# A weight ring of sixteen 1 MB units in place of eight units of 2 MB

## The reference

```
p = h @ w_in                                   # 1024 x 2560
mix = concat(attention(q, k, v), gated spatial mix, causal conv(31) + LN + silu) @ w_out   # 1024 x 1024
h = LayerNorm(alpha * h + mix)
for e in range(16):                            # top-1 group of experts, then top-2 experts of it
    out += gates[:, e:e+1] * ((silu(h @ w_gate[e]) * (h @ w_up[e])) @ w_down[e])
h = LayerNorm(alpha * h + out)
```

## Time and profile before

| | us |
|---|---|
| median of 3 runs (lowest, highest) | 730.11 (729.67, 730.49) |
| the profiled execution | 730.29 |
| its span, first to last instruction | 728.4 |
| TensorE matmul busy | 668.5 |
| VectorE busy | 281.4 |
| ScalarE busy | 141.3 |

### The profile page before, as it was taken

One profiled execution on the slowest core, in us unless ns is written; L12 is line 12 of the kernel. 1 busy time (PEld: TensorE's weight loads), 2 busy tenths in 40 slices (PEclk: granted clock), 3 DMA queues, 4 the chain that ended last, 5 costly groups with the idle time before them and its releaser, 6 DMA issues.

```text
span 728.4 us, 7319 instructions
## 1 busy us (share of the span) xinstructions
PE 668.5 (92%) x3007; PEld 327.9 (45%) x3007; DVE 281.4 (39%) x585; ACT 141.3 (19%) x280; POOL 67.9 (9%) x65
## 2 busy tenths in 40 slices
PE   7999998799999999887689999979999999997882
PEld 5644586443333543232375447846333345332331
DVE  4496668310323022130627937770120330320226
ACT  2102463131110220010121026522201122110100
POOL 1603000510000000000050310006000000000000
PEclk9999999899999999999979999998999999999997
DMA  8999535089999999999999532333999999999981
GB/s 283 345 388 416 243 119 229 1 354 409 423 422 421 421 422 420 423 420 422 393 386 405 232 142 96 136 117 142 379 421 422 421 422 422 420 422 422 421 360 60
DMA packets 48572, 240.72 MB, mean 330 GB/s; under 512 B 4428, under 2 KB 8852, under 8 KB 23956
## 3 DMA queue, kind: packets, MB, share of 16 engines
q1 hardware_dynamic: 47380, 235.97, 80.5%
q10 hardware_dynamic: 1152, 4.19, 1.5%
HBM read 239.10 MB, written 1.05 MB: 330 GB/s over the span
## 4 chain that ended last, share of the span: by engine, by line
PE 66%; DMA 18%; DVE 10%; issue 3%; POOL 2%; ACT 1%; DVEq 0%; POOLq 0%
PE bank L534 22%; PE bank L553 12%; PE bank L455 11%; DMA ring<-in_w_up 9%; DMA ring<-in_w_gate 8%; PE bank L512 5%; PE bank L469 5%; DVE mix L1278 3%; PE bank L573 3%; PE bank L610 2%; PE bank L542 1%; PE bank L682 1%; PE bank L433 1%; DVE stats L1204 1%; DVE h L1197 1%
## 5 line engine op out<-in xcount | busy, mean ns | idle before, releaser
L534 PE MATMUL bank<-ring,xe 128*64 128x512 f32 x1024 | 226.4, 594 | 18.3 <-DMA ring<-in_w_up 10.5
L534 PEld LDWEIGHTS bank<-ring,xe 128*64 128x64 f32 x1024 | 71.4, 137 | 166.6 <-issue 134.5
L553 PE MATMUL bank<-ring,area_b 128*64 128x512 f32 x512 | 113.4, 595 | 1.6 <-DVE area_b L1217 1.6
L1211 DVE TENSOR_TENSOR area_b<-area_b,bank 128x512 f32<-128x512 f32 x16 | 11.0, 688 | 261.1 <-PE bank L534 261.1
L455 PE MATMUL bank<-ring,xT_area 128*128 128x512 f32 x256 | 111.3, 593 | 0.0
L455 PEld LDWEIGHTS bank<-ring,xT_area 128*128 128x128 f32 x256 | 48.1, 190 | 57.4 <-issue 57.4
L553 PEld LDWEIGHTS bank<-ring,area_b 128*64 128x64 f32 x512 | 35.3, 137 | 68.3 <-issue 64.0
L937 POOL TENSOR_TENSOR rstd<-var_eps,half_neg 128x1 f32<-128x1 f32 x18 | 11.7, 658 | 551.9 <-DVE var_eps L1024 551.9
L1231 DVE SCALAR_TENSOR_TENSOR y_lo<-bank,slot_gate,y_hi 128x512 fp32r<-128x512 f32 x32 | 24.0, 751 | 89.1 <-ACT y_hi L858 89.1
L1278 DVE SCALAR_TENSOR_TENSOR mix<-glu,tapsT,mix 128x256 f32<-128x256 f32 x120 | 47.7, 475 | 0.0
L858 ACT ACTIVATE y_hi<-bank,slot_gate 128x512 fp32r<-128x512 f32 x32 | 22.0, 687 | 98.1 <-PE bank L553 98.1
(11 more groups left out here) (159 smaller groups left out, 568.4 us busy)
## 6 DMA issues: line engine op xcount, KB each, us to landing
ring<-in_w_gate SPq DMA_DIRECT2D x32, 2048.0 KB, 23.6
ring<-in_w_up SPq DMA_DIRECT2D x32, 2048.0 KB, 25.2
ring<-in_w_down SPq DMA_DIRECT2D x32, 2048.0 KB, 26.4
ring<-in_w_in SPq DMA_DIRECT2D x9, 2048.0 KB, 21.1
ring<-in_w_out SPq DMA_DIRECT2D x4, 2048.0 KB, 22.0
ring<-in_w_in SPq DMA_DIRECT2D x2, 1024.0 KB, 7.1
h<-in_x SPq DMA_DIRECT2D x2, 512.0 KB, 3.7
ln_par<-in_ln_mix_g ACTq DMA_DIRECT2D x2, 512.0 KB, 8.1
```

The costliest lines, as they stand in the source:

```text
L534: mm = pe.matmul(bank[2 + u % 2][e * SLOTS:(e + 1) * SLOTS, :], xe[:, k, at + e * SLOTS:at + (e + 1) * SLOTS], w[:, e, c, :], start=k == 0 ...
L553: mm = pe.matmul(bank[5 + n][e * SLOTS:(e + 1) * SLOTS, :], hidT[:, k, e * SLOTS:(e + 1) * SLOTS], w[:, e, c, n * BANK:(n + 1) * BANK], st ...
```

## The change

The unit becomes 1 MB (`UNIT = 2048`) and the ring sixteen of them; the ring's bytes stay. Each slab is two units (chunks 0 to 3 and chunks 4 to 7), each expert unit of before two units of 1024 adjacent floats for each expert and partition: 256 runs of 4 KB in each. All transfers, waits and releases are by these units, in the same order of bytes but for the second half of a slab of `w_out`, which is loaded first, as it is used first. The first slab comes in four transfers in place of two. Within `down`, units of two chunks are in use side by side, and each is released after its last product.

```diff
-UNIT = 4096
-RING = 8
-SLABS = 5 + 2
-PAIR_UNITS = 6
+UNIT = 2048
+RING = 16
+SLABS = 2 * (5 + 2)
+PAIR_UNITS = 12
...
+                to = [unit_at(n + k).rearrange("p (c n) -> p c n", c=KC // 2) for k in range(2)]
+                of = [src[:, KC // 2 * k:KC // 2 * (k + 1), :] for k in range(2)]
                 if n == 0:
-                    sp.dma_start(dst[:, :, CV:], src[:, :, CV:]).then_inc(first_half_in, 16)
-                    sp.dma_start(dst[:, :, 0:CV], src[:, :, 0:CV]).then_inc(landed[0], 16)
-                else:
-                    sp.dma_start(dst, src).then_inc(landed[n % RING], 16)
+                    for k in range(2):
+                        sp.dma_start(to[k][:, :, CV:], of[k][:, :, CV:]).then_inc(first_half_in, 16)
+                    for k in range(2):
+                        sp.dma_start(to[k][:, :, 0:CV], of[k][:, :, 0:CV]).then_inc(landed[k], 16)
+                    return
+                for k in (0, 1) if i < 5 else (1, 0):
+                    if n >= RING:
+                        sp.wait_ge(used, n - RING + (1 if i < 5 and k == 0 else 2))
+                    sp.dma_start(to[k], of[k]).then_inc(landed[(n + k) % RING], 16)
...
-                        half = u // 2 if u < 4 else u - 4
-                        if u < 4:
-                            w = (w_gate, w_up)[u % 2][l].rearrange("e (p c) n -> p e (c n)", c=KC)
+                        part = 2 * (u // 4) + u % 2 if u < 8 else u - 8
+                        if u < 8:
+                            w = (w_gate, w_up)[u // 2 % 2][l].rearrange("e (p c) n -> p e (c n)", c=KC)
                         else:
                             w = w_down[l].rearrange("e (p c) n -> p e (c n)", c=FC)
-                        src = w[:, bass.ds(first, 2), half * 2048:(half + 1) * 2048]
+                        src = w[:, bass.ds(first, 2), part * 1024:(part + 1) * 1024]
...
-                wait_unit(pe, n)
-                w = unit_at(n).rearrange("p (c n) -> p c n", c=KC)
                 for c in range(KC):
-                    mm = pe.matmul(dst[:, :], xT[:, c, b * P:(b + 1) * P], w[:, c, :],
+                    u = n + c // 4
+                    if c % 4 == 0:
+                        wait_unit(pe, u)
+                    mm = pe.matmul(dst[:, :], xT[:, c, b * P:(b + 1) * P], unit_at(u)[:, c % 4 * BANK:(c % 4 + 1) * BANK],
                                    start=c == 0, stop=c == KC - 1)
+                    if b == TB - 1 and c == 3:
+                        mm.then_inc(used, 1)
...
-                    for u in range(4):
-                        if j % GROUP == 0 and u == 2:
+                    for u in range(8):
+                        if j % GROUP == 0 and u == 4:
                             gather(g, range(4, KC))
-                        w = landed_unit(PAIR_UNITS * j + u).rearrange("p (e c n) -> p e c n", e=2, c=4)
-                        for c in range(4):
+                        w = landed_unit(PAIR_UNITS * j + u).rearrange("p (e c n) -> p e c n", e=2, c=2)
+                        for c in range(2):
...
-                    for u in range(2):
-                        w = landed_unit(PAIR_UNITS * j + 4 + u).rearrange("p (e c n) -> p e c n", e=2, c=2)
+                    for u in range(0, FC, 2):
+                        w = [landed_unit(PAIR_UNITS * j + 8 + u).rearrange("p (e n) -> p e n", e=2), None]
                         for n in range(2):
                             for c in range(2):
+                                k = u + c
+                                if n == 0 and c == 1:
+                                    w[1] = landed_unit(PAIR_UNITS * j + 8 + k).rearrange("p (e n) -> p e n", e=2)
                                 for e in range(2):
...
+                                if n == 1:
+                                    mm.then_inc(ps.used, 1)
...
-                        mm.then_inc(ps.used, 1)
```

More of the change, by code:

```diff
@@ L282, in __init__ @@
                 self.main = name == "main"
+                self.landing = 16 if self.main else 32
                 self.rounds = rounds
@@ L297, in trunk @@
             more_used = sem(f"more{l}_used")
-            more_landed = [sem(f"more{l}_landed{i}") for i in range(RING)]
+            more_both = [sem(f"more{l}_landed{i}") for i in range(RING // 2)]
+            more_landed = [more_both[i // 2] for i in range(RING)]
             o = Pass("more", more_used, more_landed, l * LAYER_UNITS + SLABS, RING, 0, ROUNDS - 1)
@@ L382, in _ @@
                 main, more = passes[l]
-                for i in range(SLABS):
-                    load_slab(l, i, l * LAYER_UNITS + i)
+                for i in range(SLABS // 2):
+                    load_slab(l, i, l * LAYER_UNITS + 2 * i)
                     if l == 0 and i == 0:
@@ L470, in product @@
                                    start=k0 == 0 and k == 0, stop=k0 == KC - 1 and k == 2)
-                    if k0 == KC - 1 and b == 0 and k == 0:
+                    if k0 == KC - 1 and b == 0 and k < 2:
                         mm.then_inc(used, 1)
@@ L495, in landed_unit @@
                     at = (ps.unit0 + k) % RING
-                    turns = rnd * (ITERS * TURNS * 16) + it * (TURNS * 16)
-                    pe.wait_ge(ps.landed[at], turns + 16 * ((ps.load0 + k) // RING + 1))
+                    turns = rnd * (ITERS * TURNS * ps.landing) + it * (TURNS * ps.landing)
+                    pe.wait_ge(ps.landed[at], turns + ps.landing * ((ps.load0 + k) // RING + 1))
                     return ring[:, at, :]
@@ L524, in gate_up @@
                     g, at = j // GROUP, (j % GROUP) * P
-                    for u in range(4):
-                        if j % GROUP == 0 and u == 2:
+                    for u in range(8):
+                        if j % GROUP == 0 and u == 4:
                             gather(g, range(4, KC))
-                        w = landed_unit(PAIR_UNITS * j + u).rearrange("p (e c n) -> p e c n", e=2, c=4)
-                        for c in range(4):
-                            k = 4 * (u // 2) + c
-                            if j % GROUP == 0 and u % 2 == 0:
+                        w = landed_unit(PAIR_UNITS * j + u).rearrange("p (e c n) -> p e c n", e=2, c=2)
+                        for c in range(2):
+                            k = 4 * (u // 4) + 2 * (u % 2) + c
+                            if j % GROUP == 0 and u // 2 % 2 == 0:
                                 nth_group("xe", g, k + 1, KC)
                             for e in range(2):
-                                mm = pe.matmul(bank[2 + u % 2][e * SLOTS:(e + 1) * SLOTS, :],
+                                mm = pe.matmul(bank[2 + u // 2 % 2][e * SLOTS:(e + 1) * SLOTS, :],
                                                xe[:, k, at + e * SLOTS:at + (e + 1) * SLOTS], w[:, e, c, :],
@@ L601, in _ @@
                 wait_xT(l, 0, TB - 1)
-                w = unit_at(u0).rearrange("p (c n) -> p c n", c=KC)
                 for k in (2, 3, 0, 1):
                     if l == 0 and k == 2:
-                        pe.wait_ge(first_half_in, 16)
-                    elif k == (2, 0)[l == 0]:
-                        wait_unit(pe, u0)
+                        pe.wait_ge(first_half_in, 32)
                     for c in range(KC):
+                        if k == (2, 0)[l == 0] and c % 4 == 0:
+                            wait_unit(pe, u0 + c // 4)
                         mm = pe.matmul(bank[4 + k // 2][:, (k % 2) * SEQ:(k % 2 + 1) * SEQ],
-                                       w[:, c, k * P:(k + 1) * P], xT[:, c, :], start=c == 0, stop=c == KC - 1)
+                                       unit_at(u0 + c // 4)[:, c % 4 * BANK + k * P:c % 4 * BANK + (k + 1) * P], xT[:, c, :],
+                                       start=c == 0, stop=c == KC - 1)
+                        if k == 1 and c == 3:
+                            mm.then_inc(used, 1)
                 mm.then_inc(used, 1)
@@ L614, in _ @@
                     setup()
-                rows_slab(u0 + 1, (0, 1))
+                rows_slab(u0 + 2, (0, 1))
                 if l == 0:
                     pe.wait_ge(setup_copied, 1)
-                rows_slab(u0 + 2, (2, 3))
+                rows_slab(u0 + 4, (2, 3))
                 pe.wait_ge(conv_step, CB * TAPS * (l + 1))
@@ L625, in _ @@
                 mm.then_inc(convT_pe, 1)
-                rows_slab(u0 + 3, (6, 7))
+                rows_slab(u0 + 6, (6, 7))
                 pe.wait_ge(rot_done, 2 * TB * (l + 1))
@@ L675, in _ @@
                 mm.then_inc(spatial_pe, 1)
-                block_slab(u0 + 4, 1, bank[5])
+                block_slab(u0 + 8, 1, bank[5])
                 for g in range(6):
@@ L786, in w_high @@
             def w_high(l, i):
-                n = l * LAYER_UNITS + 5 + i // KC
-                if i % KC == 0:
+                c = OUT_CHUNKS[i % KC]
+                n = l * LAYER_UNITS + 10 + 2 * (i // KC) + c // 4
+                if i % 4 == 0:
                     act.wait_ge(landed[n % RING], 16 * (n // RING + 1))
```

(8 more changed lines are left out.)

26 lines of the change are left out of this document (11 added, 15 removed).

## The result

The changed kernel takes 737.70 us (median of 5 runs, 737.15 to 738.20) against 730.34 for the kernel before: ratio 1.0107, 95% interval 1.0093 to 1.0121. The forecast was 736.5, and slower. The profiled execution took 737.6 with a span of 735.7 us; before it was 730.29 and 728.4.

A forecast was written before the change was run, and what follows sets the result against it. TensorE paces the mixer and first five expert pairs, the weight stream each layer's last two. Rate +5.8 and start -1.75 move the last landing +4.0; down ends +3.1, twice +6.2: 730.29 to 736.5 us, range 731.0 to 741.5.

The forecast's parts named there:

- The stream without a pause: Each layer's expert weights from unit 10 on: 38 units back to back, whose start and rate fix the layer's end.
- the term counted twice: Down's end in each layer moves from 356.28 to 359.4, +3.1 us, once per layer: +6.2.
- The rate: Expert weight stream with 4 KB runs: 2 MB take 5.13 us in place of 4.98, +5.8 us a layer.
- The line through two saturated neighbours: Per-packet plus per-byte cost, from 8 KB at 421 and 2 KB at 386 GB/s: 4 KB at 408.6 GB/s.
- The start of the stream: Early in each layer's experts, smaller units are released sooner, so the unpaused stream begins 1.75 us earlier.
- The tail: Last down: last MB lands at 356.6, three of four quarters remain, 2.65 plus 0.2 us; down ends at 359.4.
- SyncE's issues: Twice as many, 0.37 us each, hidden while the queue is filled: nothing; uncovered, 0.37 at a start, twice.
- the first slab: Program start: two more issues of 0.65 us ahead of the sg_w load cost nothing, 1.3 us if wrong.
- TensorE's added waits: At unit boundaries in the experts: more waits cost nothing where the data is there.
- near five transfers: SyncE's queue depth: about 23.6 / 4.98 transfers held, the same number of packets after the change.
- a sign against it: Everything up to layer 0's experts stays unmoved; a first 135 us that moved would prove the forecast wrong.
- The sum: Whole kernel: profiled 730.29 + 6.2 = 736.5 us, range 731.0 to 741.5; this case's chance 0.80.

The follow-up runs named there:

- the second time: The changed kernel run and profiled once more with no edit: 737.40 us, ratio 1.0110 to the kernel before.
- runs_8k: Changed kernel's 1 MB units, but one expert each in 8 KB runs, waited for and released two together: 729.87 us, ratio 1.0001 to the kernel before.
- runs_4k: 1 MB units of one expert, waits and releases two together, against the same with 8 KB runs: runs cut to 4 KB; 746.21 us.
- runs_2k: 1 MB units of one expert, waits and releases two together: gate and up in 2 KB runs, down in 4 KB; 756.46 us.
- runs_16k: Kernel before, 2 MB units, but 28 of each layer's 38 stream units hold one expert's whole matrix in 16 KB runs: 727.05 us, ratio 0.9965.
- coarse_waits: Changed kernel's transfers, but TensorE waits for and releases the experts' units two at a time: 741.55 us, ratio 1.0157 to the kernel before.
- halves: Kernel before, but four units per layer (one early, last three) come in two 1 MB transfers of 4 KB runs: 729.44 us, ratio 0.9991.

## Why the prediction was right

*What bounds it, and the unit of account.* Right. The stream without a pause and its rate set both layers' ends; the term counted twice (+3.7 and +3.2 of expert time, and +4.0 and +3.6 the second time, for +3.1 each).

*The rate.* The line through two saturated neighbours gave 408.6 GB/s and 2.566 us for 1 MB; the windows show 409 and the landings 2.56. runs_8k shows that the number of transfers has no part in it, runs_4k and runs_2k that the run's length alone does it, the 426 of runs_16k that the line goes on. By coarse_waits the term is +5.1 to +5.3 a layer for the 5.5 to 5.8 of units 10 to 45 or 47.

*The start of the stream.* This is the term that was mis-sized. The releases moved by 1.7 us as reckoned, but not the stream's end. In coarse_waits the last MB of up weights lands 205.9 us after the first gate_up (348.06 - 142.13), in the changed kernel 205.2 (348.76 - 143.57); both profiles of the changed kernel have 205.2 and 205.5 in layer 0 and 204.7 and 205.2 in layer 1, coarse_waits 205.9 and 205.8, so 0.4 to 1.1 us reach the end of the stream, 0.7 in the mean, not 1.75. In halves 1.7 at the request left 0.1 at the landing. The sum had the stream at full rate from its first packet; in the windows the units that are asked for one at a time, as they are released, move more slowly (354 GB/s in halves against 404). How much of the changed kernel's missing 1 us this makes is not shown.

*The tail.* The landing to wait for was the predicted one, with 12 of 32 instructions left, and the last MB landed 10.15 us after the last of up weights, for the 10.26 of the sum. Start and tail together gain 1.6 a layer, not 2.65; what the start does not explain of it, some 0.9, is the tail as reckoned. The rate term came out about 0.6 smaller than reckoned (5.2 for 5.8), the start about 1 smaller, and the two errors, of opposite sign, leave +3.6 for +3.1. That the forecast came this near is in part luck.

*What was set at nothing.* SyncE's issues and the first slab: right, by runs_8k, whose ratio is 1.0001 with both. TensorE's added waits: right, 32 instructions of gate_up take 7.02 us in the chains of both kernels, over two units or over four. The queue did not hold near five transfers but about seven (18.3 us from issue to landing by part 6 of the changed kernel's page, / 2.566), to no effect. The profile's first 143 us did move, which the forecast had named as a sign against it; the granted clock in the first product accounts for it.

*The sum.* 2 x 3.6 = 7.2 us of 7.4 measured in the medians; the forecast had 6.2.

*The fit of the Trainium skill* for a single transfer (DMA: Bandwidth & Descriptors, section Anatomy of one DMA), by which each transfer would bring 2.0 us of its own, did not bear here: in runs_8k halving the size of every transfer changed nothing while several were queued. The 408.7 GB/s of the Trainium skill for rows of 4 KB (same page, section iDMA fabric) agrees with the 409 of the windows.

## What to carry to other kernels

When a load stream bounds a stage, cutting its units in two is two changes: the waits and releases get finer, which gains once at the start of the stream and once at its tail, and the contiguous runs may get shorter, which costs on every byte. Cut along a dimension that keeps the run's length (runs_8k keeps the rate so; no run here joined that with finer waits throughout), or cut only the units at the tail; a rate for a run length that no trace shows can be read off the line between two that are saturated. A start that is won must still be followed to the landing that sets the end.

## What was not expected of the hardware

Runs of 16 KB are worth something over 8 KB: 426 against 421 GB/s in a mixed stretch, and 2.2 us of 729.3 in the medians. Between 17 and 26 us after the first gate_up, when the ring has just begun to be refilled, one expert's 4 KB runs moved at 339 to 346 GB/s with the engines 0.97 to 0.98 busy, where 8 KB runs had 404 and the full queue has 409 for 4 KB; the cause is open. And the granted clock in the first product differs between executions (1.00 or 0.66 over 12 to 17 us), which makes it 14.0 or 15.7 us long and moves everything after it by 1.7 us. The first gate_up lies between 140.9 and 143.6 in the ten profiles; the rest of that spread has its own low stretches, as in runs_4k, granted 0.64 over 120 to 135 us where the kernel before had 0.98. A difference of that size between two profiles has to be looked for there first.
